# Second block's attention by pairs of heads instead of head by head

## The reference, cut to what matters

```python
def banded_window_attention(q, k, v, k_ctx, v_ctx, sink):
    ...
    s_loc = jnp.einsum('bnqhgd,bnkhd->bnhgqk', qb, kw).astype(jnp.float32) * scale
    s_ctx = jnp.einsum('bnqhgd,blhd->bnhgql', qb, k_ctx).astype(jnp.float32) * scale
    ...
    valid = (jnp.abs(rel) <= WINDOW)[None] & (kpos >= 0) & (kpos < S)
    s_loc = jnp.where(valid[None, :, None, None], s_loc, NEG)
    ...
    p = jax.nn.softmax(jnp.concatenate([s_loc, s_ctx, sink_l], axis=-1), axis=-1)
    p_loc = p[..., :3 * BLOCK].astype(v.dtype)
    p_ctx = p[..., 3 * BLOCK:3 * BLOCK + L].astype(v.dtype)
    o = (jnp.einsum('bnhgqk,bnkhd->bnqhgd', p_loc, vw)
         + jnp.einsum('bnhgql,blhd->bnqhgd', p_ctx, v_ctx))
```

## Time and profile before

| what | us |
|---|---|
| median of 3 runs | 1547.3 (1545.46 to 1549.88) |
| the profiled execution: its own time | 1544.11 |
| its span, first to last instruction | 1542.0 |
| PE busy in the span | 1458.8 (95%) |
| VectorE (DVE) busy | 816.2 (53%) |
| ScalarE (ACT) busy | 633.7 (41%) |
| GpSimd (POOL) busy | 57.7 (4%) |

### The profile page before, as it was taken

One profiled execution on the slowest core, in us unless ns is written; L12 is line 12 of the kernel. 1 busy time (PEld: TensorE's weight loads), 2 busy tenths in 40 slices (PEclk: granted clock), 3 DMA queues, 4 the chain that ended last, 5 costly groups with the idle time before them and its releaser, 6 DMA issues.

```text
span 1542.0 us, 16757 instructions
## 1 busy us (share of the span) xinstructions
PE 1458.8 (95%) x6644; PEld 1140.6 (74%) x6644; DVE 816.2 (53%) x1162; ACT 633.7 (41%) x984; POOL 57.7 (4%) x46
## 2 busy tenths in 40 slices
PE   7999987889999999999989999999899999999995
PEld 5777664657888888886867777788657888888884
DVE  5565665567866666335455444436454534444334
ACT  5435555424445443335334443435343433333332
POOL 2000000002003000001000000000010000000001
PEclk9999998899999999999999999999999999999998
DMA  6422111331222224221222222103311222222221
GB/s 226 172 81 96 41 42 68 139 134 68 98 94 96 96 96 150 96 96 68 64 105 102 96 94 96 69 28 132 127 69 68 96 96 96 96 96 96 97 95 54
DMA packets 41400, 147.71 MB, mean 96 GB/s; under 512 B 4427, under 2 KB 5451, under 8 KB 40940
## 3 DMA queue, kind: packets, MB, share of 16 engines
q1 hardware_dynamic: 41324, 146.66, 26.6%
HBM read 143.23 MB, written 3.41 MB: 95 GB/s over the span
## 4 chain that ended last, share of the span: by engine, by line
PE 85%; DVE 7%; ACT 4%; issue 2%; DMA 2%; SPq 0%; DVEq 0%; ACTq 0%
PE PS L271 24%; PE PS L273 23%; PE PS L272 23%; PE PS L870 2%; PE PS L833 1%; DVE X L1445 1%; ACT whi L230 1%; DVE wlo L237 1%; PE PS L432 1%; ACT L L1003 1%; PE PS L852 1%; PE PS L526 1%; PE PS L448 1%; PE PS L542 1%; PE PS L837 1%
## 5 line engine op out<-in xcount | busy, mean ns | idle before, releaser
L237 DVE TENSOR_TENSOR wlo<-raw,whi 128x1024 fp32r<-128x1024 f32 x210 | 259.2, 1239 | 417.0 <-ACT whi L230 416.5
L271 PE MATMUL PS<-Hhi,whi 128*128 128x512 f32 x1032 | 414.8, 402 | 17.8 <-DVE wlo L237 6.0
L272 PE MATMUL PS<-Hlo,whi 128*128 128x512 f32 x1032 | 404.2, 392 | 0.0
L273 PE MATMUL PS<-Hhi,wlo 128*128 128x512 f32 x1032 | 403.9, 391 | 0.0
L230 ACT ACTIVATE whi<-raw 128x1024 fp32r<-128x1024 f32 x210 | 220.6, 1054 | 279.4 <-DMA raw<-in_w_up 121.2
L271 PEld LDWEIGHTS PS<-Hhi,whi 128*128 128x128 f32 x1032 | 194.9, 189 | 77.9 <-issue 23.2
L273 PEld LDWEIGHTS PS<-Hhi,wlo 128*128 128x128 f32 x1032 | 194.9, 189 | 42.1
L272 PEld LDWEIGHTS PS<-Hlo,whi 128*128 128x128 f32 x1032 | 195.0, 189 | 39.5 <-issue 1.2
L271 PE MATMUL PS<-Dhi,whi 128*128 128x512 f32 x352 | 136.9, 389 | 0.0
L272 PE MATMUL PS<-Dlo,whi 128*128 128x512 f32 x352 | 136.9, 389 | 0.0
L273 PE MATMUL PS<-Dhi,wlo 128*128 128x512 f32 x352 | 136.9, 389 | 0.0
(11 more groups left out here) (376 smaller groups left out, 1990.1 us busy)
## 6 DMA issues: line engine op xcount, KB each, us to landing
raw<-in_w_up SPq DMA_DIRECT2D x88, 512.0 KB, 3.4
raw<-in_w_down SPq DMA_DIRECT2D x44, 512.0 KB, 3.4
wm<-in_w_mod SPq DMA_DIRECT2D x36, 512.0 KB, 3.5
raw<-in_w_g SPq DMA_DIRECT2D x16, 512.0 KB, 4.4
mw<-in_w_mod SPq DMA_DIRECT2D x3, 2048.0 KB, 8.3
raw<-in_w_o SPq DMA_DIRECT2D x8, 512.0 KB, 3.5
raw<-in_w_out SPq DMA_DIRECT2D x8, 512.0 KB, 3.4
X<-in_x SPq DMA_DIRECT2D x4, 512.0 KB, 8.4
```

Source lines behind the costliest of these rows:

```text
L237: e.tensor_tensor(wlo[i % NS], raw[i % NS], whi[i % NS].bitcast(f32), ALU.subtract).then_inc(q["w_lo"], 1)
L271: e.matmul(o, lhs[0], rhs[0], start=first, stop=False)
L272: e.matmul(o, lhs[0], rhs[1], start=False, stop=False)
L273: return e.matmul(o, lhs[1], rhs[0], start=False, stop=last)
```

## The change

The loop becomes 19 ticks over 16 steps. A step p is now a pair of heads (both values of e) of one query block; the order is query block outside, j inside (p // 4, p % 4).

- Scores: the two heads' matmuls are issued alternately, on the lower and upper 64 rows, into banks 0-1 and 2-3. A pair takes all four banks, so a pair's scores wait for the exponentials of the pair before it.
- Softmax: one maximum over both heads' logits, one small operation for two heads where there were two, and the sink's exponential for both at once. The division is now made on the probabilities, in place (`a_scaled`, two DVE operations of 512 or 640 per pair), ahead of the transposes.
- Transposes: 8 or 10 in one run, into banks 4 to 6; one ACT copy of 1024 or 1280 per pair.
- Values: the values are PE's weights (64 columns a head), the transposed probabilities of two pairs the moving data (256 columns); the two heads go to the lower and upper 64 partitions of bank 6, columns 256 to 511. Done once for two pairs (`a_values(v)`, 8 times). The output is feature-major, so `a_back`, `O2` and `OT` fall away, and `a_out` and `a_out_lo` work on 128x256, 8 times.
- Fill: one half behind the scores (and values), one behind the transposes; 4 and 2 halves in the last two ticks.
- Modulation: `A_MOD` gives 3, 3, then thirteen times 2, then 4 and 4 operations; `acc_columns` goes ahead of values 0, 2, 4, 6 and 7, into bank 6, columns 0 to 7; the transposes of the next even pair wait for `mod_add`.
- `cchi`, `cclo` and the probabilities lie elsewhere in memory, and the rounding of `cchi` moves to tick 3.

```diff
+    A_FILL = [(1, 1)] * 16 + [(2, 2), (2, 0)]
+    A_MOD = [3, 3, 2] + [2] * 12 + [4, 4]
+    A_COLUMNS = {0: 4, 2: 5, 4: 6, 6: 7, 7: 8}
...
         for n in range(16, 36):
             if n >= 18:
-                load_to(e, ld, CH["w_f2"] + ((MOD_TICK[n - 18] + 1) * 38 // 34 + 1) // 2 + NS)
+                load_to(e, ld, CH["w_f2"] + min(1 + sum(a + b for a, b in A_FILL[:A_MOD_TICK[n - 2] + 1]) // 2, 20) + NS)
             mod_load(e, n)
...
+        def a_scores(p):
+            qb, j, k0, nl = a_geom(p)
+            flat = [PS[:, 2 * h:2 * h + 2, :].rearrange("p a b -> p (a b)") for h in range(2)]
...
+                e.wait_ge(q["a_e"], 3 * (p - 1) + 2)
+            e.wait_ge(q["rp"], 3 * j + 6)
+            qq = [Q2[64 * h:64 * h + 64, j, 128 * qb:128 * qb + 128] for h in range(2)]
+            for h in range(2):
+                e.matmul(flat[h][:, 0:128 * nl], qq[h], K2[64 * h:64 * h + 64, 128 * k0:128 * (k0 + nl)],
+                         start=True, stop=False)
+            for h in range(2):
+                for i, (o, m) in enumerate(masks):
+                    e.matmul(flat[h][:, o:o + 128], identb, m, start=False,
+                             stop=i == len(masks) - 1)
+            for c0, c1 in [(0, 256)] if nl == 2 else [(0, 128), (128, 256)]:
+                for h in range(2):
+                    last = e.matmul(flat[h][:, 128 * nl + c0:128 * nl + c1], qq[h], KC[64 * h:64 * h + 64, c0:c1],
+                                    start=True, stop=True)
...
+        def a_turn(p):
...
+            e.wait_ge(q["a_n"], 2 * p + 2)
...
+            if p >= 2 and p % 2 == 0:
+                e.wait_ge(q["a_olo"], p // 2)
+                if p // 2 - 1 in A_COLUMNS:
+                    e.wait_ge(q["mod"], MOD_NTH[A_COLUMNS[p // 2 - 1]])
+            for h in range(2):
+                for i in range(n):
+                    o = 640 * h + 128 * i
+                    last = e.transpose(tp[:, o:o + 128], PB[p % 2][h][:, 128 * i:128 * i + 128], ident)
...
+        def a_values(v):
+            qb, j, k0, nl = a_geom(2 * v)
+            e.wait_ge(q["a_pt"], 2 * v + 2)
+            if v in A_COLUMNS:
+                acc_columns(A_COLUMNS[v], 6, 0)
+            for i in range(nl + 2):
+                for h in range(2):
+                    w = V2[:, k0 + i, 64 * h:64 * h + 64] if i < nl else VC[:, i - nl, 64 * h:64 * h + 64]
+                    last = e.matmul(PS[64 * h:64 * h + 64, 6, 256:512], w, PT2[:, h, :, 128 * i:128 * i + 128],
+                                    start=i == 0, stop=i == nl + 1, skip_group_check=True)
...
+        for t in range(18):
+            if t < 16:
+                a_scores(t)
+            if t % 2 and t >= 3:
+                a_values((t - 3) // 2)
+            for _ in range(A_FILL[t][0]):
                 fill()
+            if 0 <= t - 1 < 16:
+                a_turn(t - 1)
+            for _ in range(A_FILL[t][1]):
+                fill()
...
+        def a_exps(p):
...
+            e.wait_ge(q["a_st"], 5 * p + 3)
+            if p >= 2:
+                e.wait_ge(q["a_tr"], p - 1)
+            for h in range(2):
+                act(PB[p % 2][h][:, 0:n], flat[h][:, 0:n], ACT.Exp, "a_e", bias=anm[:, p % 2, h:h + 1],
+                    scale=0.125, accum_out=asum[:, p % 2, h:h + 1])
+            act(ask[:, p % 2, :], ask[:, p % 2, :], ACT.Exp, "a_e")
...
+            act(PT2[:, :, p % 2, 0:n], tp[:, :, 0:n], ACT.Copy, "a_pt")
...
+        for t in range(19):
...
+            if t % 2 and 3 <= t < 18:
+                a_out((t - 3) // 2)
+            if t < 16:
+                a_exps(t)
+            for _ in range(A_FILL[t][0] if t < 18 else 0):
                 fill()
+            if 0 <= t - 1 < 16:
+                a_turned(t - 1)
...
+        def a_stats(p):
...
+            e.tensor_reduce(amx[:, i, :], flat[:, :, 0:n], AX.X, ALU.max, negate=True).then_inc(q["a_st"], 1)
...
+        def a_scaled(p):
...
+            e.reciprocal(arc[:, i, :], atot[:, i, :]).then_inc(q["a_st"], 1)
+            e.wait_ge(q["a_st"], 5 * p + 5)
+            for h in range(2):
+                x = PB[i][h][:, 0:n]
+                ts(x, x, arc[:, i, h:h + 1], 1.0, ALU.mult, ALU.mult, "a_n")
...
+            if t < 16:
+                a_stats(t)
+            if t % 2 and 3 <= t < 18:
+                a_out_lo((t - 3) // 2)
+            for _ in range(A_FILL[t][0] if t < 18 else 0):
                 fill()
+            if t < 16:
+                a_scaled(t)
+            for _ in range(A_FILL[t][1] if t < 18 else 0):
+                fill()
+            if t < len(A_MOD):
+                mod_part(A_MOD[t])
```

More of the change, by code:

```diff
@@ L106, in build @@
     dmx, dsum, drs, drl = (small[:, 160 + 8 * i:168 + 8 * i].rearrange("p (s e) -> p s e", e=2) for i in range(4))
-    amx, anm, asum, ask, atot, arc = (small[:, 192 + 4 * i:196 + 4 * i] for i in range(6))
+    amx, anm, asum, ask, atot, arc = (small[:, 192 + 4 * i:196 + 4 * i].rearrange("p (s e) -> p s e", e=2)
+                                      for i in range(6))
     rtok = small[:, 216:220]
@@ L180, in build @@
     GT = at("GT", "M", 0, [128, 16, T])
[L181 to L184, removed]
+    PB = [[at("PB00", "E", 0, [128, 640]), at("PB01", "E", 2560, [128, 640])],
+          [at("PB10", "E", 5120, [128, 640]), at("PB11", "K", kk + 1024, [128, 640])]]
+    PT2 = at("PT2", "G", 0, [128, 2, 2, 640])
     ABhi = at("ABhi", "H", 0, [128, 4, 4, 256], f32r)
@@ L828, in a_scores @@
                 e.wait_ge(q["bm_cc"], 3)
                 e.wait_ge(q["qk2_ev"], 4)
+            else:
+                e.wait_ge(q["a_e"], 3 * (p - 1) + 2)
             e.wait_ge(q["rp"], 3 * j + 6)
[L831 to L835, removed]
@@ L849, in a_turn @@
+        def a_turn(p):
+            n = a_geom(p)[3] + 2
+            tp = PS[:, 4:7, :].rearrange("p a b -> p (a b)")
+            e.wait_ge(q["a_n"], 2 * p + 2)
+            if p:
+                e.wait_ge(q["a_pt"], p)
             else:
                 e.wait_ge(q["rp"], 13)
-            for i in range(n):
-                last = e.transpose(tp[:, 128 * i:128 * i + 128], P2b[s % 2][:, 128 * i:128 * i + 128], ident)
-            last.then_inc(q["a_tr"], 1)
[L855 to L870, removed]
-            last.then_inc(q["a_pv"], 1)
@@ L1310, in fill @@
                 act(GT[:, n - 4, :], PS[:, 7, :], ACT.Copy, "g_ev")
[L1312 to L1344, removed]
+        def a_exps(p):
+            n = 128 * (a_geom(p)[3] + 2)
+            flat = [PS[:, 2 * h:2 * h + 2, :].rearrange("p a b -> p (a b)") for h in range(2)]
+            e.wait_ge(q["a_st"], 5 * p + 3)
[5 more added lines that the diff above has]
+            act(ask[:, p % 2, :], ask[:, p % 2, :], ACT.Exp, "a_e")
@@ L1346, in scalar_program @@
         fill()
         fill()
-        left = 38
-        for tick in range(37):
-            if tick == 6:
+        for t in range(19):
+            if t == 3:
                 e.wait_ge(q["l_c2"], 48)
-                e.wait_ge(q["mcol"], MOD_NTH[10])
                 act(cchi, ccs, ACT.Copy, "const_hi")
[L1354 to L1357, removed]
+            if t % 2 and 3 <= t < 18:
[3 more added lines that the diff above has]
+            for _ in range(A_FILL[t][0] if t < 18 else 0):
@@ L1796, in vector_program, with a_out_lo @@
+        def a_out_lo(v):
+            qb, j, k0, nl = a_geom(2 * v)
+            cols = slice(128 * qb, 128 * qb + 128)
+            e.wait_ge(q["a_ohi"], v + 1)
+            tt(ATlo[:, j:j + 2, cols], PS[:, 6, 256:512].rearrange("p (a b) -> p a b", a=2),
+               AThi[:, j:j + 2, cols].bitcast(f32), ALU.subtract, "a_olo")
+            if v in A_COLUMNS:
+                mod_add(A_COLUMNS[v], 6, 0)
         fill()
         fill()
-        left = 38
-        for tick in range(37):
-            if tick == 6:
+        for t in range(19):
+            if t == 3:
@@ L1814, in vector_program @@
-            if tick in MOD_TICK:
-                mod_part(2)
+            if t < 16:
[3 more added lines that the diff above has]
+            for _ in range(A_FILL[t][0] if t < 18 else 0):
+                fill()
+            if t < 16:
+                a_scaled(t)
+            for _ in range(A_FILL[t][1] if t < 18 else 0):
+                fill()
+            if t < len(A_MOD):
+                mod_part(A_MOD[t])
         e.wait_ge(q["mod"], MOD_NTH[8])
```

129 lines of the change are left out of this document (40 added, 89 removed).

## The result

The changed kernel takes 1507.51 us in the median (1504.13 to 1508.69), against 1547.32 before; the ratio is 0.9738 with an interval of 0.9716 to 0.976. The forecast was 1509.8. The profiled execution took 1508.69, its span is 1506.5.

A forecast was written before the change was run, and what follows sets the result against it. PE was taken to bound the attention loop. 47.8 us less PE work and old waits, minus 10.3 of new waits, gave 37.5 saved: profiled 1544.1 to 1506.6, plus 3.2 for the median, 1509.8; range 1500 to 1522.

The forecast's parts named there:

- The free second head: Scores: a pair costs what one head did plus the second head's masks, 1.49 edge, 1.84 middle; 23.3 us saved.
- The rival of the in-order reading, half beside each other: Scores and values: two heads' matmuls only half overlap on PE, losing 15.5 us, 1525 in all; chance 0.04.
- the fully serial one: Scores and values: the two heads' matmuls do not overlap on PE at all, 1541 us; chance 0.01.
- Values by the run, not by the chunk: Values: a run of chunks pays the fixed 0.15 once, 1.87 at the edge, 2.30 in the middle; 13.5 us saved.
- The bound of 0.58 a chunk: Values: if each chunk pays the fixed part, they take 20.9 us and the saving is 9.3.
- PE's work: Attention loop: PE's work falls by 42.6 us; together with the old order's 5.2 of waits, 47.8 less.
- Transposes at nothing: Transposes ahead of the values: 144 of the same kind before and after, so 0 saved.
- Fill: Fill in the loop: 38 halves in both, entries behind scores or values fall from 34 to 18, 1.6 us saved.
- The new waits: PE's waits for modulation sums, `Flo`, and the last ticks' copy and columns: 10.3 us, bounds 4 and 16.
- The clock: Loop: clock 1.00 forecast; a rival had waits of 3 us lower it and values pay each chunk, 1522; chance 0.18.
- The score banks: Next scores need the exponentials 3.8 us after scores end; PE has 6.9 of other work, so no wait, 3 spare.
- The rest of the kernel: Behind the loop, the Fourier products: PE is the bound before and after, taken as unchanged.

The follow-up runs named there:

- Without neighbours: Changed kernel with each head's scores issued as context, keys, masks, one head after the other, so masks stand between the heads: 1523.23 us, ratio 0.9838.
- both edits: Changed kernel with DVE's modulation sums ahead of a tick's second fill half and PE's modulation columns behind the values: 1497.15 us, ratio 0.9666.
- early sums: Changed kernel with only DVE's modulation sums moved ahead of a tick's second fill half: 1499.25 us, ratio 0.9682, loop 174.3 us.
- the scores apart: Changed kernel with all of head 0's score matmuls (keys, masks, context), then all of head 1's: 1520.14 us, ratio 0.9819.
- the last orders: Kernel with sums ahead and columns behind values, its pairs of scores reordered to context, keys, masks: 1493.15 us, ratio 0.9671.

## Why the prediction was right, point by point

- **The free second head** (1.49 and 1.84 a pair of scores) held: 1.48 and 1.82. Without neighbours the pair costs 2.89 to 3.01, at the edge 2.32 to 2.43. The rival of the in-order reading, half beside each other, and the fully serial one fall.
- **Values by the run, not by the chunk** (1.87 and 2.30) held: 1.88 and 2.31 (865.66 to 867.97). The bound of 0.58 a chunk, 4.2 us, was not needed.
- **PE's work** came out 2.1 us lower than forecast, by errors of both signs. The table sums PE's timeline of the loop from start to start, before and with both edits, where the clock is full:

| us | before | with both edits | change | forecast |
|---|---|---|---|---|
| scores | 49.8 | 26.6 | -23.2 | -23.3 |
| values | 31.2 | 16.8 | -14.4 | -13.5 |
| transposes | 18.7 | 14.5 | -4.2 | 0 |
| transposes back | 3.9 | 0 | -3.9 | -4.2 |
| fill | 109.1 | 109.5 | +0.4 | -1.6 |
| columns | 4.0 | 4.6 | +0.5 | 0 |
| together | 216.6 | 171.9 | -44.7 | -42.6 |

- **Transposes at nothing** is the term with the largest error. The same 144 cost less in long runs: ten take 1.01, where two runs of five took 1.28, and eight 0.79.
- **Fill** did not gain its 1.6. Its entries behind scores and values became fewer, but each of the 16 runs of transposes is now followed by fill, which then starts with 0.08 more, and that had been left to the range.
- **The new waits**, 10.3, are 9.1: 0.73 for `Flo` (1.1), 2.50 and 3.53 for the long columns (3.1, 3.3), 0.49, 0.50 and 0.64 for the short ones (0.7 each), 0.69 for bank 7 (0.7). Moving the sums, or the columns, removes them, which shows the mechanism and not only the place.
- **The clock** was left out of the central sum and put into a rival, "two such places 3 us". There were two such places, and 3.3 us. The forecast's "clock 1.00" was wrong: a wait forecast at 3 us should have brought its clock loss with it. It was made up for elsewhere: the busy time at full clock was put 2.1 us too high, the waits 1.2 too high, and the clock's loss 3.3 too low.
- **The score banks** have time, as counted: in the middle step whose scores end at 855.5 the exponentials end 3.9 later (forecast 3.8), and the next scores start at 862.33, 3 us after that. Doubling each maximum shows the same. DVE and ACT, counted at 6.4 and 5.0 in a middle tick, are busy for 5.1 and 4.5 from 849.7 to 859.4, 5.4 and 4.8 from 868 to 877.9.
- **The rest of the kernel** is 526.2 us behind the loop, to the tenth what it was.

So the mechanism was right term by term where it mattered, but that 37.2 us against 37.5 came out so close is in part luck: errors of 2 to 3 us cancel. Not settled: why the loop with early sums is 0.3 us shorter than waits and clock account for, why the part ahead of the loop varies, and what makes the clock fall.

## What to carry to other kernels

Two heads of 64 rows cost TensorE what one does here, apart from the masks, as long as the two are next to each other in its program; keep whatever uses all rows at the ends of the run, not in its middle. After a change that shortens the bound engine's tick, look at what used to come just in time behind it (here a sum that was last in DVE's order and first in PE's), and where a trace of the kernel shows the clock falling behind such waits, count that in: here waits of 2.5 and 3.5 us cost 1.6 more each. No waits at all are no promise of a full clock, as the run without neighbours shows. The gain of the change was 37 us; moving the sums by one place in DVE's program was worth 10 more.

## What the runs showed of the chip that was not expected

- Matmuls on different row halves, or with outputs in different column halves, also overlap where two heads only touch in the program: at the border of scores by the records at 846.96 to 847.40, at the border of values for about two chunks (840.62 to 841.54).
- The length of a wait does not tell whether the clock falls to half behind it, for some 3 us or twice that. With every maximum twice it fell behind waits of 1.52 (951.25) and 1.71 (866.15), but not behind one of 1.72 (911.42; 1.00 up to 918). With the scores apart it fell behind 1.19 (824.02), without neighbours behind 0.77 (824.47) and behind none (956.98). What decides it is open.
- A change of tile shape between all-row and 64-row matmuls costs PE time: of the last orders, one such change fewer for a pair saves 0.20 us and two fewer 0.32.
- Transposes in a run of eight or ten cost 0.10 each, at a granted clock of 1.00, against 0.13 in the runs of five of the earlier trace rows.
